# State space layer of a decoder step: channels on partitions, products of head pairs in column groups, z and the steps' chain inside the projection pipeline

## The reference, cut to what matters

```python
u = h @ w_in                                  # 1024 -> z 2048 | xbc 3072 | dt 32
xbc = silu(causal_dwconv(ext, conv_w, conv_b))      # x 2048, B 4x128, C 4x128
dt = softplus(dt_raw + dt_bias);  a = -exp(a_log)
# per chunk of 128 tokens, 4 groups g of 8 heads e, headdim p = 64, state n = 128
cum = cumsum(dt * a)
w = (C B^T)[..., None] * exp(cum_t - cum_s) * dt_s          # s <= t
y = w @ x + (C @ state) * exp(cum) + d_skip * x
state = state * exp(cum_end) + sum_s exp(cum_end - cum_s) dt_s B_s x_s
y = rmsnorm(y * silu(z), norm_w per group) @ w_out
```

## Time and profile before

| | us |
|---|---|
| median of 3 runs | 3364.31 (3359.61 to 3364.52) |
| the profiled execution, its own time | 3363.42 |
| its span in the trace | 3361.8 |
| TensorE busy | 2825.5 (84%) |
| last xbc matmul starts | 1977.74 |
| next block (weights of the chunks) starts | 2244.26 |
| first chunk starts | 2389.29 |
| output product of chunk 0 / 1 / 7 / 8 starts | 2451.55 / 2499.03 / 2810.66 / 2846.68 |

### The profile page before, as it was taken

How to read it: one execution, slowest core, us unless ns; L and a number is a source line. 1 busy time by engine, 2 the same in 40 slices (tenths; PEclk the granted TensorE clock), 3 DMA queues, 4 the chain that set the end, 5 groups by cost and what they waited for, 6 DMA issues and landing times. The chain is left out here.

```text
span 3361.8 us, 42138 instructions
## 1 busy us (share of the span) xinstructions
PE 2825.5 (84%) x16534; PEld 2223.9 (66%) x16534; DVE 1568.0 (47%) x2711; ACT 822.6 (24%) x1492; POOL 589.3 (18%) x436
## 2 busy tenths in 40 slices
PE   5997856665998989988889978978589999699889
PEld 5996633334766779956689966755455554499566
DVE  3999624443554430045355643105576775300353
ACT  3223413332221322222233221101122221221221
POOL 2222210001331321102222200000121222221012
PEclk8998978898998989989999989987799999799999
DMA  2311540003552002213022221126533321121151
GB/s 84 95 45 53 181 148 0 0 1 129 175 173 80 1 26 74 83 75 126 5 83 96 84 99 62 70 65 225 142 88 101 95 74 15 32 69 39 60 203 46
DMA packets 237204, 277.40 MB, mean 83 GB/s; under 512 B 44870, under 2 KB 183815, under 8 KB 231316
## 3 DMA queue, kind: packets, MB, share of 16 engines
q1 hardware_dynamic: 217234, 186.84, 18.3%
q0 software_dynamic: 16384, 75.77, 6.3%
q10 hardware_dynamic: 3456, 12.98, 1.0%
HBM read 230.51 MB, written 45.47 MB: 82 GB/s over the span
## 5 line engine op out<-in xcount | busy, mean ns | idle before, releaser
L305 PE MATMUL pp<-HH,WS_part 128*128 128x352 f32 x1824 | 589.1, 323 | 0.0
L303 PE MATMUL pp<-HH,WH 128*128 128x352 f32 x1344 | 436.4, 325 | 30.2 <-POOL WS_part L444 30.2
L304 PE MATMUL pp<-HT_part,WH 128*128 128x352 f32 x1344 | 434.4, 323 | 0.0
L305 PEld LDWEIGHTS pp<-HH,WS_part 128*128 128x128 f32 x1824 | 345.3, 189 | 0.0
L303 PEld LDWEIGHTS pp<-HH,WH 128*128 128x128 f32 x1344 | 254.3, 189 | 32.0 <-POOL WS_part L444 32.0
L2658 PE MATMUL OP<-oWO,YT 128*128 128x512 f32 (+1 forms) x576 | 252.5, 597 | 3.3 <-DVE XE L2785 3.3
L304 PEld LDWEIGHTS pp<-HT_part,WH 128*128 128x128 f32 x1344 | 254.5, 189 | 0.0
L444 POOL TENSOR_TENSOR WS_part<-WS,WH 128x1024 fp32r<-128x1024 f32 x56 | 143.1, 2555 | 504.1 <-ACT WH L395 504.1
L816 DVE SCALAR_TENSOR_TENSOR CV<-GX,cw,CV x360 | 215.9, 676 | 0.0
L2658 PEld LDWEIGHTS OP<-oWO,YT 128*128 128x128 f32 (+1 forms) x576 | 103.8, 182 | 144.0 <-issue 140.1
L1976 DVE TENSOR_REDUCE xmx<-xS 128x4 f32<-128x1024 f32 x16 | 19.5, 1219 | 377.4 <-PE xS L1937 377.4
(11 more groups left out here) (490 smaller groups left out, 5498.0 us busy)
## 6 DMA issues: line engine op xcount, KB each, us to landing
WS<-x_w_qg SPq DMA_DIRECT2D x32, 512.0 KB, 4.0
HT<-cache_mem_k SPq DMA_DIRECT2D x16, 1024.0 KB, 8.1
HT<-cache_mem_v POOLq DMA_DIRECT2D x16, 1024.0 KB, 9.0
CBt<-cum_scratch SPq DMA_DIRECT2D x8, 2048.0 KB, 10.0
xbc_scratch<-oACC ACTq DMA_DIRECT2D x24, 528.0 KB, 2.7
WS<-o_w_in SPq DMA_DIRECT2D x24, 512.0 KB, 3.9
XT<-xbc_scratch SPq DMA_DIRECT2D x8, 1536.0 KB, 7.6
WS<-e_w_in SPq DMA_DIRECT2D x20, 512.0 KB, 4.0
```

The costliest lines, as they stand in the source:

```text
L303: nc.tensor.matmul(out, wh, xh, start=start, stop=False)
L304: nc.tensor.matmul(out, wh, xl, start=False, stop=False)
L305: return nc.tensor.matmul(out, wl, xh, start=False, stop=stop)
```

## The change

Everything of the mixer moves to channels on partitions.

1. **z** becomes 16 more column blocks of the same `project` pipeline (4 jobs of 4), each [128 channels, 1056 tokens]; silu on ACT, stores by ACT's queue to a scratch with channels first. `z_project` and its tiles go.
2. **The steps' chain** goes into the same block: three small loads ahead of the weight loads on SP, the two small ACT instructions ahead of ACT's loop, the step matmuls after the xbc job (two groups) and after the first z job (one), the chain on DVE behind the convolution, its ACT parts inside z's evacuations.
3. **`odd_states`** goes: its transposes stand between the z jobs.
4. **Chunks**: x is still transposed, but DVE reads it from PSUM with the step factor (no copy on ACT); the differences go from DVE to ACT (32 Relu with a bias per partition); `EC`, the cumulative sums by channel, is a new load of 1 MB per chunk and one exponential; C x state has state as stationary operand (16 matmuls of 128 columns for 4 of 512); the products within the chunk have x stationary (64 columns) and the weights moving (128 columns), the two heads of a pair in the two column halves of the array; d_skip is 16 instructions on DVE for one on POOL and one on DVE; the norm sums squares with 16 matmuls by ones, then mean, Sqrt on ACT, reciprocal and one multiply on DVE, in place of the 16 transposes of Y, POOL's powers and 8 instructions on DVE; the norm's gain is multiplied into `WO` once, in the first chunk (16 instructions on ACT); `XT` is loaded after the gate, behind `CB` and `EC`.
5. **Samples**: 16 transposes and a copy bring `YS` to channels. Two small strided loads (`Dc`) replace `Db`.

```diff
@@ project: SP, PE, ACT, DVE
+            if "sync_before" in extra:
+                extra["sync_before"](sp)
...
+                if "tensor_after" in extra:
+                    extra["tensor_after"](pe, plan.index(n0))
...
+            if "scalar_before" in extra:
+                extra["scalar_before"](act)
...
+            if "vector_before" in extra:
+                extra["vector_before"](dve)
@@ odd_conv_project
+        def z_store(act, z):
+            act.wait_ge(p_ev[z % 2], 3 * (n2 + XB // 2 + z // 2 + 1))
+            act.dma_start(z_d[z], ZT[:, z % 2, :]).then_inc(g_st[z % 2], 16)
+        def z_out(m):
+            def out(act, j, k, g, ps, ready):
+                z = 4 * m + k
+                if g == 0:
+                    if (m, k) == (1, 1):
+                        act.wait_ge(t_own.sem, 2)
+                        nc.scalar.activation(e[:], e[:], ACT.Exp, scale=-1.0).then_inc(t_x, 1)
+                    if (m, k) == (1, 3):
+                        act.wait_ge(t_own.sem, 3)
+                        nc.scalar.activation(ln[:], u[:], ACT.Ln).then_inc(t_x, 1)
+                    if (m, k) == (2, 2):
+                        act.wait_ge(t_own.sem, 14)
+                        nc.scalar.activation(dec[:], cum[:, TP + TS - 1:TOK:TS], ACT.Exp).then_inc(t_x, 1)
...
+                ready()
+                a, b = GROUPS[g]
+                return nc.scalar.activation(ZT[:, z % 2, a:b], ps[:, 0:GRP], ACT.Silu)
+        def small_loads(sp):
+            sp.dma_start(WD[:], w[:, :, SI + XBC:]).then_inc(t_l, 16)
+            sp.dma_start(bias[:], A["o_dt_bias"].rearrange("o h -> h o")).then_inc(t_l, 16)
+            sp.dma_start(al[:], A["o_a_log"].rearrange("o h -> h o")).then_inc(t_l, 16)
+        def between(pe, job):
+            if job == 0:
                 pe.wait_ge(t_wl, 1)
+                steps(pe, 0)
+                steps(pe, 1)
+            elif job == 1:
+                pe.wait_ge(t_ev, 1)
+                steps(pe, 2)
+            elif job < 4:
+                tails(pe, 2 * job - 4)
+                tails(pe, 2 * job - 3)
...
+        project(c, [(col, XB // 4, 4, act_step, on_dve)] + [(z_col(m), 1, 4, z_out(m), None) for m in range(4)], HT, HH, 4,
+                {"sync_before": small_loads, "scalar_before": small_high, "vector_before": small_low, "tensor_after": between,
+                 "tensor": finish, "vector": chain, "sync": stores, "scalar": all_stored})
@@ ssd_chunks, SP: after CB
+                        sp.wait_ge(r_ev, n * 8 - 4)
+                    for a in range(2):
+                        sp.dma_start(EC[64 * a:64 * a + 64, :, 0:T], cum_c[a][:, bass.ds(n * P, T)].partition_broadcast(64))\
+                            .then_inc(r_xc, 16)
+                    if not first:
                         sp.wait_ge(r_yg, n)
+                    sp.dma_start(XT[:, :, 0:T], xbc_d[:, :, bass.ds(n * P, T)].rearrange("n p t -> p n t")).then_inc(r_x, 16)
@@ PE
                     if first:
-                        pe.wait_ge(r_w, 64)
+                        pe.wait_ge(r_dx, NX)
...
-                            m = nc.tensor.matmul(V[g][:, :], XT[:, NX + 4 + g, :], ST[:, g * 512:(g + 1) * 512],
-                                                 start=True, stop=True)
+                            pe.wait_ge(r_xd, n * 4 + g + 1)
+                            for k in range(4 * g, 4 * g + 4):
+                                m = nc.tensor.matmul(V[g][:, (k % 4) * P:(k % 4 + 1) * P], ST[:, k * P:(k + 1) * P], XT[:, NX + 4 + g, :],
+                                                     start=True, stop=True)
...
-                            m = nc.tensor.matmul(U[g % 2][R, e * SP_:(e + 1) * SP_], CB[R, h, R], XD[R, h * SP_:(h + 1) * SP_],
-                                                 start=True, stop=True)
+                        for k in range(4):
+                            for a in range(2):
+                                h = g * HP + 2 * k + a
+                                m = nc.tensor.matmul(U[g % 2][64 * a:64 * a + 64, k * T:(k + 1) * T], XD[R, h * SP_:(h + 1) * SP_], CB[R, h, R],
+                                                     start=True, stop=True, tile_position=(0, 64 * a), skip_group_check=True)
...
-                            t = nc.tensor.transpose(U[q % 2][:, k * T:(k + 1) * T], Y[R, kt * P:(kt + 1) * P], ident[R, R])
+                    for k in range(NX):
+                        m = nc.tensor.matmul(U[0][:, (k // 4) * T:(k // 4 + 1) * T], ones[:], Z[:, k, R], start=k % 4 == 0, stop=k % 4 == 3)
+                    m.then_inc(r_sg, 1)
@@ ACT
+                        for h in range(g * HP, (g + 1) * HP):
+                            ins = nc.scalar.activation(CB[R, h, R], CB[R, h, R], ACT.Relu, bias=cus[R, h:h + 1], scale=-1.0)
+                        ins.then_inc(r_seg, 1)
...
+                    act.wait_ge(r_xc, n * 32 + 32)
+                    nc.scalar.activation(EC[:, :, R], EC[:, :, R], ACT.Exp).then_inc(r_ex, 1)
+                    if first:
+                        act.wait_ge(r_s, 96)
+                        act.wait_ge(r_w, 64)
+                        for k in range(NX):
+                            nc.scalar.activation(WO[:, k, :], WO[:, k, :], ACT.Copy, scale=onw[:, k:k + 1]).then_inc(r_dx, 1)
                     act.wait_ge(r_yg, n + 1)
+                    act.wait_ge(r_z, n * 16 + 16)
+                    nc.scalar.activation(Z[:, :, R], Y[:, :, R], ACT.Square).then_inc(r_sq, 1)
                     if not first:
                         out(n - 1, P)
+                    act.wait_ge(r_ms, n + 1)
+                    nc.scalar.activation(RS[:, 0:4 * T], RS[:, 0:4 * T], ACT.Sqrt).then_inc(r_rs, 1)
@@ DVE
+                    for k in range(NX):
+                        ins = N.scalar_tensor_tensor(out=Y[:, k, R], in0=XT[:, k, R], scalar=Dc[:, k:k + 1], in1=Y[:, k, R],
+                                                     op0=ALU.mult, op1=ALU.add)
...
                     if not first:
+                        out_mean(n - 1, P)
+                    dve.wait_ge(r_sg, n + 1)
+                    N.tensor_scalar(RS[:, 0:4 * T], U[0][:, 0:4 * T], 1.0 / 512, EPS, ALU.mult, ALU.add).then_inc(r_ms, 1)
                     if not first:
                         out(n - 1, P)
+                        dve.wait_ge(r_om, n * 2)
+                    dve.wait_ge(r_rs, n + 1)
+                    v(N.reciprocal(RS[:, 0:4 * T], RS[:, 0:4 * T]))
+                    N.tensor_tensor(YT[:, :, R].rearrange("p (g k) t -> p g k t", g=4), Y[:, :, R].rearrange("p (g k) t -> p g k t", g=4),
+                                    RS[:, 0:4 * T].rearrange("p (g t) -> p g t", g=4).unsqueeze(2).to_broadcast([P, 4, 4, T]),
+                                    ALU.mult).then_inc(r_ye, 1)
```

More of the change, by code:

```diff
@@ new lines, in steps, with tails @@
+        def steps(pe, g):
+            a, b = GROUPS[g]
+            for kt in range(KT):
+                m = split_mm(zb[g % 2][0:SH, 0:GRP], (WDH[:, kt, :], WDL[:, kt, :]), (HH[:, kt, a:b], HL[:, kt, a:b]),
+                             kt == 0, kt == KT - 1)
+            m.then_inc(t_mm, 1)
+        def tails(pe, r):
+            if r < 2:
+                pe.wait_ge(t_ev, 3)
+                pe.wait_ge(t_g, 1)
+            else:
+                pe.wait_ge(o_te, r - 1)
+            for n in range(4 * r, 4 * r + 4):
+                t = nc.tensor.transpose(zb[r % 2][0:27, (n % 4) * P:(n % 4 + 1) * P], G[:, n, :], ident[:])
+            t.then_inc(o_tp, 1)
@@ L2457, in _ @@
                 for i, T in enumerate(TILES):
-                    for v, src in enumerate((x, cum)):
-                        t = nc.tensor.transpose(tp[v][0:T, i * SH:(i + 1) * SH], src[:, i * P:i * P + T], ident[0:SH, 0:SH])
+                    t = nc.tensor.transpose(zb[v][0:T, i * SH:(i + 1) * SH], src[:, i * P:i * P + T], ident[0:SH, 0:SH])
                 t.then_inc(t_tp, 1)
-                pe.wait_ge(t_x, 4)
-                pe.wait_ge(t_l, 64)
-                for n in range(16):
-                    m = nc.tensor.matmul(ep[:, n * NB:(n + 1) * NB], hsel[:, n, :], dec[:], start=True, stop=True)
@@ new lines, in stores, with all_stored @@
+        def stores(sp):
+            sp.wait_ge(t_own.sem, 14)
+            sp.dma_start(cum_d, cum[:]).then_inc(t_st, 16)
+            sp.dma_start(hsel, A["c_head"]).then_inc(t_l, 16)
+            sp.wait_ge(o_te, 6)
+            sp.dma_start(O[8][0, 0], st[0:3, :]).then_inc(o_out, 16)
+            sp.dma_start(O[9][0].rearrange("b k c -> (b k) c"), st[3:27, :]).then_inc(o_out, 16)
+            sp.wait_ge(o_out, 32)
+            sp.wait_ge(t_st, 16)
+        def all_stored(act):
+            z_store(act, 15)
+            stored(act)
+            for k in range(2):
+                act.wait_ge(g_st[k], 128)
@@ L2613, in _ @@
             def _(sp):
+                cum_c = cum_d.rearrange("(k a) t -> a k t", a=2)
                 def chunk(n, T, sample, first):
-                    if not first:
```

(12 more changed lines are left out.)

410 lines of the change are left out of this document (152 added, 258 removed).

## The result

The changed kernel took 3394.89 us (median of 4 runs) where the kernel before, beside it, took 3361.96: a ratio of 1.0099, with a 95% interval of 1.0081 to 1.0116. Run once more beside the experiments it took 3385.33 us (6 runs) against 3362.76, a ratio of 1.0075 (1.0053 to 1.0097). So it is slower by 0.75 to 1%, 23 to 33 us; the prediction was 3358 us, within 3338 to 3383.

The account below looks back on a forecast made before the run. TensorE, busy 84% of the span, was taken as the bound. Terms: -58.4 (projection through sample stage), +27 (first chunk), +21 (seven steady chunks), +4 (last) = -6.4 us from 3364.3, so 3358 us, range 3338 to 3383.

Parts of the forecast that it names:

- the sum's first part: Projection with z and steps, weights block and sample stage together: 58.4 us less, between -62 and -54.
- The two strided `Dc` loads: Weights block: one more issue and its landing in a block waiting for all loads, +1 us (0.4 to 2).
- C: Rival, steady chunks: clock falls in the gap and again in the products, 3.5 us more each, 3383 us; chance 0.19.
- E: Rival, transfers: 512-byte rows slow the loads so x is late, or conflict slows chunk 0; 3372 to 3385; chance 0.07.
- The pipeline: Projection with z, steps and tails: TensorE never held up, the 32 passes at the block's end start 61.1 us earlier.
- Chunk 0: First chunk: TensorE waits for ScalarE's scalings, then for chunk 1's x; +27 us, between +18 and +35.
- Steady chunks: Seven later chunks: faster products, but a 6 us TensorE gap at the norm; period 54.3 us, +3.0 each, +21.
- The wait at a change of tiling mode: Chunk products: engine drain at two mode changes per chunk, estimated 3 us in seven chunks; nothing added.
- Last chunk: Last chunk's norm: ones passes, reciprocal and scale make its output product start later, +4 us (0 to 7).
- What I gave 0: Sample stage: its transposes end under the last state's store, 0 us, or 3 us if that cover were gone.
- D: Rival, chunks: ScalarE's activation table loads fall behind their wait, +9 us, 3367 us; chance 0.06.
- B: Rival, steady chunks: the gap costs less, chunks add 0 to +10 us, time 3337 to 3347 us; chance 0.20.

Follow-up runs that it names:

- the padded run: Changed kernel with a 32-byte tile added ahead of the projection's weight tiles, restoring their earlier offset within 64 bytes: 3385.1 us.
- The two cures: Two separate runs on the changed kernel: ScalarE's output-weight scalings ahead of its first wait in chunk 0, 3371.2 us; chunk 0's XT loaded first, 3378.6 us.
- the filling passes: Changed kernel plus 6 unused 512-column matrix passes in TensorE's gap ahead of the first output half of every chunk but the first: 3377.8 us, ratio 1.0043.

## Why the prediction was wrong

The sign was wrong, and one term turned it: the small loads of the sum's first part. It is 16.4 of the 38.6 us between the forecast of -6.4 and the +32.2 us between the two profiled spans. The rest is spread over the items 2, 3, 5 and 6.

1. **The two strided `Dc` loads: the step that failed.** I took "one issue and its landing in a block that waits for all of them: +1 us (0.4 to 2)". They cost 17.4 us, and with contiguous loads in their place the block was back at 6.3 us. I had looked at the number of loads and not at their form, and no row of before showed a strided load broadcast over partitions. The nearest, `onw`, has single elements without a broadcast and lands fast, so a bound from the nearest rows would have missed too. With 17.4 in place of 1 the sum is +10.0 us: slower, and near the rivals C and E in time, for none of their reasons.

2. **The pipeline: right in kind, 5.3 us too good.** -54.1 for -59.4. TensorE was never held up, as argued. Up to the last 32 passes of the block it lost 6.7 us on the forecast. The token groups are 4.7 of them, 3.885 us for 3.845 in 120 groups (shown by the padded run); a z block then takes 11.66 us, just over the 11.6 that I had named as a sign of being wrong. The step matmuls are 1.9: the earlier trace rows counts 15 of them in 2 us, and I divided by that, but such a row also counts those that begin before or end after it. In both kernels they follow one another every 0.16 us, 11.5 us for 72, where I took 9.6. The first token group, at the low clock for longer, is 1.0. The first pass gave 0.5 back: it comes 9.14 us behind the block's first load for 7.98, 1.2 us later, where I had allowed 1.7 for the three small loads. Together that is 7.1 us; the 0.4 us too much aren't traced. From the start of the 32 passes the block ended in 4.6 us for 6.1, which gave 1.4 back. The run with the old chunks behind the new pipeline keeps the whole gain.

3. **Chunk 0: right in kind, 7 us short.** +34.1 for +27, still inside 18 to 35, with both waits where they were forecast. x landed 20.5 us into the chunk for 18.5; the products ended 0.3 us later than that alone makes them; and x of chunk 1 landed 22.1 us behind the products for 18.5. I took 290 GB/s from 1.5 us in chunk 0 and let nothing but `CB`, `EC` and `XT` share it. In the first 20.5 us of the chunk the trace has a mean of 248 GB/s, 5.1 MB for my 4.72: the rate was lower, and z's load, issued at 2370.61, took its share before x was there. Between the issue of chunk 1's `CB` and its transposes the mean is 250. Transposes from there took 6.0 us for 4.8. The two cures show that the losses are ScalarE's scalings (19.0 us) and the order of the loads (10.6 us).

4. **Steady chunks: right, the split in part by luck.** +21.0 for +21, period 54.3 us for 54.3, gap 6.37 us for 6, ended by `YT`, products 3.9 us for 4.1. But it isn't 3.0 us seven times: the first period grew by 6.2 us and the other six by 2.5 on average, since the 51.3 us that I compared with is a mean of one short period (47.5) and six of 51.6 to 53.3. The clock's part was 2.8 us where I took 1.9, and the filling passes show it to be the gap's. That my figure for the products came from the attention's column pairs, same shapes, was sound; the reason I had in mind for it, that pairs overlap, explains 1.1 of the 5.3 us only. The wait at a change of tiling mode, which I had left out of the sum, doesn't show: C x state (2690.00, 3.73 us) and the products behind it (2693.67) follow without a gap.

5. **Last chunk: right.** +5.2 for +4.

6. **What I gave 0.** The sample stage moved +5.9 us in the first execution and -5.4 in the second, and its clock with it. That is most of the 12.9 us between their spans. The stages ahead of the projection added 2.1 and 3.1 us, inside their spread. My bound of 0.2% was too narrow: the two ratios measured for this kernel lie 0.24% apart, with intervals that overlap.

7. **The rivals.** D is refuted: the table loads run ahead of the waits in the chunks too, as the table's row had it. In the changed kernel's trace the root's load, issued behind the output's squares, is over before `RS` comes (load from 2715.69 to 2716.97, root at 2719.28), and so is the exponential's (2722.25 to 2723.53, instruction at 2728.48). C, the clock at the products, did not occur: all 64 passes and the new state run at the full clock. E, transfers slower, holds for chunk 0 in part, and nowhere else. B did not occur.

## What to carry to other kernels

A block that waits for all its loads lasts as long as the slowest of them, however small it is: 4 KB with a stride of two over broadcast partitions took 15.7 us where contiguous it took 3.1. When work is folded together, price what then stands alone on the path: the first chunk lost 34 us, and the version with the scalings in front of a wait and another order of the four loads, among its other cures, had 28 of them back; seven steady chunks lost 21. A gap of TensorE costs its length and then the clock behind it: 6.4 us of gap were 9.2 us of period, and with a gap shorter by 2.1 us the period was shorter by 1.1 to 2.8.

## What the runs showed of the hardware that was not expected

- A load of 4 KB with 4-byte elements at a stride of 8 bytes, broadcast to 64 partitions, lands in 15.7 us, with its elements neighbouring in 3.1 us (of two such loads issued together), and a load of 128 KB queued behind it on the same engine took 5.49 us to issue.
- The same matrix passes (128 x 128 weights, 352 columns) take 1% longer with the weight tiles at a multiple of 64 bytes than 32 bytes past one: 3.885 us against 3.845 for 24 passes, in eleven executions of the one kind (504.0 to 504.3 us for the projection) and two of the other (501.1 and 501.2). That the offset within 64 bytes is the cause, and not another effect of the move by 32 bytes, wasn't tried.
- Two streams of 64-column weight tiles in the two column halves: 0.061 us a pass in alternation, 0.078 us one half after the other.
- The same sample stage took 130.7 to 144.6 us in the fourteen profiled executions, with the granted clock from 0.83 to 0.70. What decides the clock there stays open.
